# One transformer layer with 32 routed experts: two loops over each expert's token blocks, and a fourth weight buffer for every other gate matrix

## What is computed

```python
h = x + mix                                       # 320 x 2048
xn = rmsnorm(h, norm_ffn)
g_idx = argmax(xn @ w_rg + b_rg)                  # 1 of 4 groups
top_p, top_i = top_k(softmax((xn @ w_re + b_re)[g_idx]), 2)
gate = g_p * top_p / sum(top_p)
for e in range(32):                               # rows of xn that chose e
    hb = silu(xb @ w_gate[e]) * (xb @ w_up[e])    # 2048 -> 512
    out[rows] += (hb @ w_down[e]) * gate          # 512 -> 2048
y = rmsnorm(h + out, norm_final)
```

## Time and profile before

| what | value |
|---|---|
| median of three runs | 1521.75 us (1521.0 to 1523.71) |
| the profiled execution: its time, its span | 1520.95 us, 1518.7 us |
| mean granted clock of TensorE | 0.925 |
| bytes moved in the span | 473.91 MB, 312 GB/s on average |
| TensorE, VectorE, ScalarE busy | 88%, 39%, 23% |
| expert stage | from 569.73 us to the last add at about 1507 us |

### The profile page before, as it was taken

One profiled execution on the slowest core, in us unless ns is written; L12 is line 12 of the kernel. 1 busy time (PEld: TensorE's weight loads), 2 busy tenths in 40 slices (PEclk: granted clock), 3 DMA queues, 4 the chain that ended last, 5 costly groups with the idle time before them and its releaser, 6 DMA issues.

```text
span 1518.7 us, 22119 instructions
## 1 busy us (share of the span) xinstructions
PE 1343.1 (88%) x8510; PEld 714.1 (47%) x8511; DVE 596.3 (39%) x1183; ACT 347.2 (23%) x591; POOL 32.0 (2%) x41
## 2 busy tenths in 40 slices
PE   5999999999999999788888888888889988887885
PEld 4989999566666663232222322322323322223221
DVE  6335444044574443242243234224324422332344
ACT  5332322123453322111111111111211111111113
POOL 1000000000000000000000000000000000000000
PEclk9999999999999989999898888988989989889887
DMA  9454451023353368999999999999989999999994
GB/s 323 132 166 137 161 167 60 10 70 111 92 180 112 132 284 358 411 434 433 430 430 435 432 430 432 434 431 430 433 362 397 432 434 431 432 432 433 431 432 180
DMA packets 69607, 473.91 MB, mean 312 GB/s; under 512 B 9516, under 2 KB 46512, under 8 KB 55680
## 3 DMA queue, kind: packets, MB, share of 16 engines
q1 hardware_dynamic: 68640, 470.85, 76.0%
q0 software_dynamic: 832, 2.48, 0.5%
q10 hardware_dynamic: 96, 0.02, 0.0%
HBM read 469.97 MB, written 3.38 MB: 312 GB/s over the span
## 4 chain that ended last, share of the span: by engine, by line
PE 52%; DMA 41%; DVE 3%; issue 2%; ACT 1%; SPq 0%; DVEq 0%; ACTq 0%
DMA ring<-in_w_down 41%; PE ps L879 11%; PE ps L579 5%; PE ps L580 5%; PE ps L581 5%; PE ps L864 3%; PE ps L640 2%; PE ps L667 2%; PE ps L730 2%; PE ps L731 2%; PE ps L732 2%; PE ps L743 2%; PE ps L841 2%; PE ps L661 1%; PE ps L870 1%
## 5 line engine op out<-in xcount | busy, mean ns | idle before, releaser
L1561 DVE TENSOR_TENSOR hreg<-ps,hreg 128x512 f32<-128x512 f32 (+1 forms) x396 | 239.6, 679 | 290.2 <-PE ps L890 290.2
L864 PE MATMUL ps<-ring,mix 128*32 128x512 f32 x2112 | 281.6, 681 | 30.4 <-DMA ring<-in_w_up 17.9
L879 PE MATMUL ps<-ring,mix 128*32 128x512 f32 x1056 | 166.2, 787 | 60.6 <-DMA ring<-in_w_down 53.1
L890 PE MATMUL ps<-mix 32*128 32x512 f32 (+1 forms) x792 | 156.3, 612 | 26.4 <-ACT mix L1234 25.6
L1191 ACT COPY mix<-ps 128x512 f32<-128x512 f32 x66 | 70.5, 1069 | 448.3 <-PE ps L864 448.3
L864 PEld LDWEIGHTS ps<-ring,mix 128*32 128x32 f32 x2112 | 74.6, 122 | 207.8 <-issue 177.8
L579 PE MATMUL ps<-xT_hi,w_hi 128*128 128x320 f32 (+1 forms) x528 | 165.5, 313 | 4.9 <-DVE w_lo L1299 2.9
L580 PE MATMUL ps<-xT_lo,w_hi 128*128 128x320 f32 (+1 forms) x528 | 164.5, 312 | 0.0
L581 PE MATMUL ps<-xT_hi,w_lo 128*128 128x320 f32 (+1 forms) x528 | 164.4, 311 | 0.0
L1299 DVE TENSOR_TENSOR w_lo<-ring,w_hi 128x1024 fp32r<-128x1024 f32 (+1 forms) x66 | 76.7, 1205 | 105.9 <-ACT w_hi L1006 105.9
L879 PEld LDWEIGHTS ps<-ring,mix 128*32 128x32 f32 x1056 | 40.0, 138 | 160.7 <-issue 103.9
(11 more groups left out here) (259 smaller groups left out, 1187.5 us busy)
## 6 DMA issues: line engine op xcount, KB each, us to landing
ring<-in_w_gate SPq DMA_DIRECT2D x31, 4096.0 KB, 22.1
ring<-in_w_up SPq DMA_DIRECT2D x31, 4096.0 KB, 23.7
ring<-in_w_down SPq DMA_DIRECT2D x31, 4096.0 KB, 23.7
ring<-in_w_in SPq DMA_DIRECT2D x32, 1024.0 KB, 8.2
ring<-in_w_o SPq DMA_DIRECT2D x16, 1024.0 KB, 6.8
hreg<-in_x_prompt SPq DMA_DIRECT2D x4, 1024.0 KB, 6.2
ring<-in_w_up SPq DMA_DIRECT2D x2, 2048.0 KB, 11.6
ring<-in_w_gate SPq DMA_DIRECT2D x2, 2048.0 KB, 8.2
```

What stands on the lines that cost most here:

```text
L864: last = pe.matmul(ps[r:r + B, bank, :], x[:, k % 4, k // 4, :], w[:, k, :], start=k < 4, stop=k >= KC - 4)
L879: last = pe.matmul(ps[B * j:B * (j + 1), 4, :], h[:, c, :], w[:, c, 512 * j:512 * j + 512], start=c == 0, stop=c == 3)
L890: pe.matmul(ps[0:tn, COMB_BANKS[u % 8], :], gates[r, t0:t0 + tn], rows[r, :], start=True, stop=True).then_inc(full_sem, 1)
L1561: dve.tensor_tensor(h, ps[0:tn, COMB_BANKS[u % 8], :], h, ALU.add).then_inc(signal, 1)
```

## The change

Buffers. A fourth buffer of 32 KB a partition, `gate_b`, takes the gate weights of odd experts; it lies over mix, ckv and the first part of cq, which are free by then. For that, the router weights move from cq to krt, the biases to the end of const, the small tiles of the expert stage into work, const, krt and the rest of cq, and the last gain into ring slot 0.

Loops. `extra_blocks` and its buffers are gone. Every expert is two loops over its blocks: the first makes gate, gather, fold, up, fold and transpose for each block and keeps each block's hT in `hTs`; the second makes the transpose of the gates, down and combine for each. ScalarE copies one block's hT from `hTs` to a fixed place ahead of down. `tables` row 0 now holds the number of the expert's first block, row 1 its count. The program's loop on TensorE holds an even and an odd expert in one turn.

Loads. SyncE issues gate 1 into `gate_b` when the normed tokens are ready (`hg_ready`), ahead of the routing. Then for each expert: up when all of the last expert's up matmuls are done, down when all of its down matmuls are done, and behind that the gate of the expert one further, without a wait of its own. The last expert's down is loaded in four pieces, each with its own semaphore, and `down` waits for each piece. `norm_final` is loaded when the last of them has landed. The router loads go behind the reload of x, and VectorE scales them with the second quarter of the output.

```diff
@@ SyncE @@
-            sp.wait_ge(routed, 4)
-            with sp.Fori(1, NE) as e:
-                used = sp.value_load(tables[0:1, 3, bass.ds(e, 1)], min_val=1, max_val=65)
-                for m in range(3):
-                    sp.wait_ge(weights_used, e * 3 + (m + 1 - 3))
-                    sp.wait_ge(extra_used[m], used)
-                    w = a[("w_gate", "w_up", "w_down")[m]][0, bass.ds(e, 1)].rearrange("a b c -> (a b) c")
-                    sp.dma_start(ring[:, 2 * m:2 * m + 2, :].rearrange("p s n -> p (s n)"), rows_of(m, w)).then_inc(slot_full[2 * m], 16)
+            sp.wait_ge(hg_ready, 12)
+            sp.dma_start(gate_b[:, :], rows_of(0, a["w_gate"][0, 1])).then_inc(gate_b_full, 16)
+            sp.wait_ge(routed, 2)
+            def up_down_next(e, dst, signal):
+                before = sp.value_load(tables[0:1, 0, bass.ds(e, 1)], min_val=1, max_val=NE + 20)
+                sp.wait_ge(up_done, before)
+                sp.dma_start(ring[:, 2:4, :].rearrange("p s n -> p (s n)"), expert_rows("w_up", 1, e)).then_inc(slot_full[2], 16)
+                sp.wait_ge(down_done, before)
+                sp.dma_start(ring[:, 4:6, :].rearrange("p s n -> p (s n)"), expert_rows("w_down", 2, e)).then_inc(slot_full[4], 16)
+                sp.dma_start(dst, expert_rows("w_gate", 0, e + 1)).then_inc(signal, 16)
+            with sp.Fori(1, NE - 2, 2) as e:
+                up_down_next(e, gate_a, slot_full[0])
+                up_down_next(e + 1, gate_b[:, :], gate_b_full)
...
+            for c in range(4):
+                sp.dma_start(ring[:, 4 + c // 2, D * (c % 2):D * (c % 2 + 1)],
+                             rows_of(2, a["w_down"][0, NE - 1])[:, D * c:D * (c + 1)]).then_inc(down_last[c - 1] if c else slot_full[4], 16)
@@ GpSimd @@
-            pool.wait_ge(hg_ready, 12)
-            pool.dma_start(gain, a["norm_final"]...
+            pool.wait_ge(down_last[2], 17)
+            pool.dma_start(gain_last, a["norm_final"]...
@@ TensorE @@
+            def expert(e, odd):
+                first = pe.value_load(tables[0:1, 0, bass.ds(e, 1)], min_val=0, max_val=NE + 20)
+                count = pe.value_load(tables[0:1, 1, bass.ds(e, 1)], min_val=1, max_val=MAXB)
+                with pe.Fori(0, count) as k:
+                    it = first + k
+                    pe.wait_ge(xg_ready, it + 1)
+                    pe.wait_ge(comb_added, first * 12 + 6)
+                    gate_full(e, odd)
+                    gate_or_up(xg, 0, odd, 2).then_inc(gate_done, 1)
+                    pe.wait_ge(comb_added, first * 12 + 8)
+                    pe.wait_ge(pick_ready, it + 2)
+                    gather(pickr, 0, gathered)
+                    pe.wait_ge(h_copied, it * 2 + 1)
+                    pe.wait_ge(hT_ready, it + 1)
+                    fold(0).then_inc(folded, 1)
+                    matrix_full(1, e)
+                    gate_or_up(xg, 1, odd, 4).then_inc(up_done, 1)
+                    pe.wait_ge(h_copied, it * 2 + 2)
+                    pe.wait_ge(silu_ready, it + 1)
+                    fold(1).then_inc(folded, 1)
+                    pe.wait_ge(g_copied, it + 2)
+                    pe.wait_ge(comb_added, first * 12 + 12)
+                    gathered_T(gsb, 1, transposed)
+                tail = pe.value_load(tables[0:1, 2, bass.ds(e, 1)], min_val=0, max_val=16)
+                after = first + count
+                with pe.Fori(0, count) as k:
+                    it = first + k
+                    pe.wait_ge(hT_ready, after + 1)
+                    pe.wait_ge(comb_added, it * 12 + 12)
+                    pe.wait_ge(gates_ready, it + 1)
+                    gates_T(gpick, gt_full)
+                    pe.wait_ge(h_picked, it + 1)
+                    down(hT, e, tail + 1).then_inc(down_done, 1)
+                    pe.wait_ge(xg_ready, after + 1)
+                    pe.wait_ge(gt_copied, it + 1)
+                    pe.wait_ge(y_copied, it + 1)
+                    combine(gT, yb, comb_full, comb_added, it * 12 + 12)
@@ ScalarE, second loop @@
+                    act.wait_ge(hT_ready, after + 1)
+                    act.copy(hT, hTs[:, bass.ds(k, 1), :].rearrange("p b q -> p (b q)")).then_inc(h_picked, 1)
```

More of the change, by code:

```diff
@@ L256, in trunk_layer_kernel @@
         gate = work[:, w0 + 252:w0 + 258].rearrange("p (i k) -> p i k", i=3)
-        dest, rank, high, place, placex = (
-            work[:, w0 + 258 + 6 * k:w0 + 264 + 6 * k].rearrange("p (i k) -> p i k", i=3) for k in range(5))
+        rank, place, shift = (work[:, w0 + 258 + 6 * k:w0 + 264 + 6 * k].rearrange("p (i k) -> p i k", i=3) for k in range(3))
         w0 += 288
@@ L423, in late_loads @@
             sp.wait_ge(psum_full, full(f"K{H - 1}_1"))
+            sp.dma_start(gain, a["norm_ffn"].to_broadcast([P, D])).then_inc(s_gffn, 16)
+            sp.wait_ge(psum_full, full(f"PV{H - 1}"))
+            sp.wait_ge(s_stage, 64)
+            sp.wait_ge(ssq_full, 4)
+            for i, (t0, tn) in enumerate(TILES):
+                sp.dma_start(xtile[0:tn, i, :], x_src[i]).then_inc(s_xagain, 16)
             sp.dma_start(wr[:, :, 0:G], a["w_router_group"][0].rearrange("(c p) e -> p c e", p=P)).then_inc(s_router, 16)
@@ L963, in _ @@
-            for m in range(3):
-                pe.sem_inc(extra_used[m], 1)
+            def expert(e, odd):
[35 more added lines that the diff above has]
+                    combine(gT, yb, comb_full, comb_added, it * 12 + 12)
@@ L965, in _ @@
+            for c in range(3):
+                pe.sem_inc(down_last[c], 1)
             keep_clock(3, 5)
@@ L969, in _ @@
             gathered_T(gsb, 1, transposed)
-            pe.wait_ge(routed, 4)
-            expert(0, slice(0, 1), True)
-            with pe.Fori(1, NE) as e:
-                expert(e, bass.ds(e, 1), False)
+            pe.wait_ge(routed, 2)
+            with pe.Fori(0, NE - 1, 2) as e:
+                expert(e, False)
+                expert(e + 1, True)
         @block.scalar
@@ L1533, in _ @@
             link(dve.tensor_reduce(rank, prod, AX, ALU.add))
-            dve.scalar_tensor_tensor(place, eid, float(B), rank, ALU.mult, ALU.add)
-            link(dve.tensor_scalar(high, rank, float(B), -1.0e6, ALU.is_ge, ALU.mult))
-            link(dve.tensor_tensor(place, place, high, ALU.add))
+            link(dve.scalar_tensor_tensor(place, eid, float(B), rank, ALU.mult, ALU.add))
             def matches(link, where, eq):
```

332 lines of the change are left out of this document (121 added, 211 removed).

## The result

The changed kernel takes 1526.12 us (median of 16 runs, 1522.18 to 1529.14), the kernel before, run beside it, 1523.15 (16 runs, 1520.44 to 1523.95). The ratio is 1.0022, with an interval of 1.0015 to 1.0029: 3.4 us slower, just past the 0.2% that the prediction called the limit of what can be told. The forecast was 1521.8 in a range of 1517.0 to 1527.5. The profiled execution took 1525.93 us, its span is 1523.8 (before 1518.7), so the two traces differ by 5.1 us; the mean granted clock is 0.932 for 0.925.

The account below looks back on a forecast made before the run. The prediction took the expert stage to be bound by its weight stream at 432 GB/s. Terms -5.5 + 0 + 6.9 - 1.3 + 0 = +0.1 us on 1520.95 gave 1521.05, with 0.8 for the median 1521.8; range 1517.0 to 1527.5.

Parts of the forecast that it names:

- What bounds the kernel: Expert stage: bound by bytes at 432 GB/s; only the stream's gaps, its start and what follows its end can change.
- Term 1: Start of the expert stage: gate 1 loads early, but up 1 waits for up 0 to be used; -5.5 us.
- a sign of being wrong: Start of the expert stage: a hole in the stream of over 8 us would show the forecast wrong.
- Term 2: Even expert rounds: 1.1 to 1.8 us more on TensorE, covered by the stream's 29.1 us an expert; 0.
- Term 3: Expert 19, the one with two blocks: the stream loses 16.1 us in place of 9.2; +6.9 us.
- Term 4: The end: the last down, loaded in four pieces, ends 4.1 us behind its landing, against 5.4 before; -1.3 us.
- Term 5: Router weights behind the x loads: a W_O piece comes later, but a cover of 4 us hides it; 0.
- C: Expert loop: it doesn't fit and its code is fetched again each turn; 57 us more, 1579; chance 0.02.
- B: First expert rounds: a wait for newly jumped-to code ahead of up 0's issue, up to 6.3 us, 1528; chance 0.15.
- its second form: Two-block expert: the adds or ScalarE's table loads make it 3 us dearer; chance 0.05.
- A: End and expert 19: the pieces bite and the clock stays up; -5.0 us, 1516.8; chance 0.22.

Follow-up runs that it names:

- The first experiment: The changed kernel, but SyncE issues the gate of expert e+1 first, ahead of up e and down e, for each expert; 1529.38 us, ratio 1.0044.
- gate 1 late: The changed kernel, but gate 1 is issued when gate 0 has been used, not when the normed tokens are ready; 1530.66 us, ratio 1.0052.
- one load: The changed kernel with the last expert's down weights in one load of 4 MB in place of four of 1 MB; 1525.01 us, ratio 1.0025.
- the fastest: The changed kernel, but gate e+1 issued first for e = 1 to 6 and 20 to 26, second-loop transpose and down behind seven adds, not twelve; 1507.63 us.

## Why the prediction was right where it was

The time lies in the forecast's range, 4.3 us above the forecast and 0.02% past its line for no change. Of the 4.3 us, 1.4 are the kernel before, whose median was 1521.75 when the forecast was made and 1523.15 beside the changed one; the change itself was forecast at +0.1 us and came to +3.4. By its steps:

- **What bounds the kernel: right, but for the end.** 432 GB/s between the gaps in both kernels, and closing its gaps, at the start and at expert 19, is what made the faster kernels. What it left out is the end: the last down's distance from the one before must be more than TensorE's own round. The first experiment shows that. In the changed kernel this distance is three matrices, 29.1 us, and the point bites only when TensorE is cold: in its trace down 30 and gate 31 took 6.13 and 6.58 us for 3.64, the last two downs are 30.4 us apart, and the last one starts 1.9 us behind the stream.
- **Term 1, -5.5 us: right in kind, too large.** This is the step that failed in the profiled pair. The hole with up 1 behind up 0 is there, but it is 9.7 us long (576.5 to 586.2), over the 8 us that the forecast had named as a sign of being wrong. Up 0 started at 581.5, not 577.2, and the stream counts from 586.2 - 9.7 = 576.5 in place of 571.9. Behind it, to 668 us, it runs at 428 GB/s, 81.9 x 4 / 432 = 0.8 us of gaps where the forecast had 0.5: 577.3 for 572.4. The count of the kernel before has the 0.2 us from 574.0 to 574.2 in it twice, so that it is 577.7: -0.4 us in this execution. Of the 4.3 us at up 0, 1.0 is new work, of which the forecast had priced 0.2 for two table reads: from the first gather to the first gate it is 6.01 us where it was 5.00, with 1.73 us of issue for 0.72, in the traces of all eleven kernels with the two loops. Nearly all the rest is the clock: the six matmuls of `keep_clock` ahead of the gather took 4.54 us for 2.84, the gate 5.29 for 3.64. In the eleven traces the gate ran warm in four and `keep_clock` in seven; in both traces of the kernel before both were warm. The new idle time ahead of the gate may have a part in its being cold more often; no run separates the two.
- **Term 2, 0: right, and its number nearly so.** Four downs of the changed kernel, none of which waited for its weights, are 26.6, 27.2 and 24.9 us apart:

```profile
1186.66 5.34 PE L910 MATMUL ps<-ring,work 128*32 128x512 f32 x32 [0.16 <-issue]
...
1213.29 3.64 PE L910 MATMUL ps<-ring,work 128*32 128x512 f32 x32 [0.20 <-ACT work L1215]
...
1240.44 3.64 PE L910 MATMUL ps<-ring,work 128*32 128x512 f32 x32 [0.20 <-ACT work L1215]
...
1265.36 5.34 PE L910 MATMUL ps<-ring,work 128*32 128x512 f32 x32 [0.20 <-ACT work L1215]
```

The third round is warm from end to end, as the 23.3 us before were: 1.6 more, for the forecast's 1.1 to 1.8. Each of the other two has one cold run in it, the down of 5.34 us and a gate of 5.39. The round is still hidden by the 29.1 us of the stream, but with a cold run in it the cover is 2 us, and where TensorE is behind the stream, after expert 19 and at the end, the longer round counts.
- **Term 3, +6.9: right mechanism.** In the two traces 15.6 - 9.2 = +6.4. By the two kernels without a second block it is +9.3, good to 3 us. The two holes are where the forecast has them: 124.9 x 54 / 432 = 15.6 us in all for its 16.1, of which the second is 12.5 (1153.0 to 1165.5) for its 13.2. The size moves from trace to trace: the stretch ran at 378 GB/s in the changed kernel and at 363 and 362 in two variants that differ from it elsewhere only (gate 1 late, one load), 19.9 and 20.2 us lost. The clock goes with it. From down 18 to the second down are seven gates, ups and downs; two of the seven were cold in the changed kernel's trace and four in that of gate 1 late, 5.0 to 6.4 us each for 3.64. With one load it is two again, but there the two runs ahead of them, down 17 and gate 18, took 6.54 us each for 4.92 and 5.34, and TensorE came to down 18 behind its weights. The forecast took one of expert 19's own as cold. The profiled execution may so have been a mild one, and the term sized some 2 us low; by intervals of 3 us that isn't shown.
- **Term 4, -1.3: the number came out by luck.** From the end of the stream to the last multiply it was 16.4 us and is 1511.89 - 1497.05 = 14.8, which is -1.5. But both sides of the forecast's difference were low by nearly the same amount. Its 5.4 for the kernel before doesn't follow from its own row: down starts 1.8 us behind the last byte and takes 5.34, which is 7.1. And the last down of the changed kernel ended 1498.97 + 3.64 - 1497.05 = 5.6 us behind the stream, not 4.1, since it started 1.9 us late. Nor did the pieces bring the gain: the last down took 3.64 us here and 5.34 in the kernel before, which alone is 1.7, and with a single load the median is the same. The gain of the last norm landed 5.7 us after its issue, below, and was hidden by 7 us.
- **Term 5, 0: right**, shown by the run with the router loads moved, within the 2 us that its interval can tell.
- **Rivals.** C fell: the queues show no code fetched, below. B's wait of up to 6.3 us for code didn't come; 1.0 us of new issue at the first gate did, and its second form, a dearer expert 19, did in part: together they put the time on the slower side. A fell: the second down stayed cold wherever all twelve adds stood ahead of it, and the pieces saved nothing.

The medians and the traces share the difference out unlike. By the kernels without a second block, everything but term 3 is worth -5.9 us, where the forecast had -6.8 (-5.5 and -1.3), and term 3 is worth +9.3, where it had +6.9: off by 0.9 and 2.4 us to the slow side, inside what these intervals can tell. In the profiled pair the steps add up as -0.4 + 6.4 - 1.5 = +4.5. The distance of the last multiplies is 1511.89 - 1506.87 = +5.0; most of the rest lies between 1230 and 1490 us, where the changed kernel ran at 431 GB/s for 432, 0.6 us. The medians differ by 3.0 only, since the profiled execution before, 1520.95, was 2.2 us below the median of the sixteen beside the changed kernel.

The load of the last norm's gain, and the queues from 650 to 1480 us as in the earlier trace rows:

```profile
ring<-in_norm_final POOLq DMA_DIRECT2D x1, 1024.0 KB, 5.7
```

Issued when the weights are in, with nothing beside it, the 1 MB took 5.7 us from issue to landing (11.9 before). The Trainium skill's estimate of 4.4 us, from DMA: Bandwidth & Descriptors, section on the anatomy of one DMA on the gpsimd path, is 1.3 us below it; neither would have reached the multiply. The rule on taken branches, from the Trainium skill, Runtime: NRT & Kernel Launch, Instruction fetch mechanics, is not borne out by the new loop either, one turn of which has 668 matmuls and weight loads (334 for an expert of one block):

```profile
q1 hardware_dynamic: 12078, 351.74, 98.6%
```

This one queue is all that moved between 650 and 1480 us, with two experts' code and two inner loops in each turn. The same holds for the other two-loop kernels but the fastest, whose list for SyncE is longer: there one packet of instructions moved on another queue.

## What to carry to other kernels

In a stage bound by its stream, these runs say, a buffer more adds no bytes; it is a reserve, and it is worth something only if it is still empty when the consumer falls behind, and gets filled then. Choose the order of the loads by that: plain while the consumer waits, ahead where it is late, and plain again before the end, since whatever is loaded ahead brings the last piece closer to the one before it than the consumer can follow (here 19.4 us for a round of 26.6). And when a data-dependent case gets a loop of its own, price the chain through its iterations (here twelve adds between two downs), not only its instructions.

## What was not expected of the hardware

- Kernels with the same code up to a place have the clock low at different places before it. The first 32 gate matmuls took 3.64 us in some traces and 5.2 to 5.3 in others, with the same waits ahead of them, and the first matmuls of W_O 0.47 or 0.77. A cold run of 32 matmuls costs 1.3 to 2.9 us, so of stage lengths read from one trace a difference below some 2 us per cold stretch says nothing.
- The `keep_clock` matmuls (L835), which bridge the routing, took 4.54 us in the traces of the changed kernel and three variants and 2.84 in those of the other seven: they too run at whichever level they find. The cold stretch moves as a whole. Where the eight such matmuls before them took 3.70 us, the six and the gate behind were cold (four traces); where the eight took 4.9 to 5.0, only the gate was (three); where they took 6.4 to 6.5, neither was (four).
- ScalarE now has 66 table loads of 1.28 us, busy time 439.9 for 347.2 us, two of them in every block; in the rows of expert 0 and 19 none is what TensorE waits for longest. A kernel without them was not tried.
